# v with keys on partitions: block transposes on VectorE and moves between quadrants, in a two-layer encoder trunk

## The reference

```python
h = rms_norm(x, g); z = h @ w_in          # 1024 -> 3712
aq, ak, av, ag, bq, bk, bv, bg, ca, cb, cg = jnp.split(z, splits, axis=-1)
ya = neighbourhood_attention(aq, ak, av, rpb) * silu(ag)       # 4 heads, 8 x 16 window of an 8 x 64 grid
yb = dilated_attention(rotary(bq), rotary(bk), bv) * silu(bg)  # 6 heads, 3 dilated windows
yc = conformer_conv(ca, cb, ...) * silu(cg)                    # depthwise conv of 31 taps, 384 channels
x = x + concat([ya, yb, yc]) @ w_out
# an attention: p = softmax(q @ k.T * scale + bias); out = p @ v
```

## Time and profile before

| | us |
|---|---|
| median of 3 runs | 542.46 (540.92 to 544.98) |
| the profiled execution, its own time | 542.2 |
| its span, first to last instruction | 540.2 |
| busy: TensorE, VectorE, ScalarE, GpSimd | 528.5, 361.1, 287.3, 135.3 |
| granted clock of TensorE, mean | 0.999 of full speed |

### The profile page before, as it was taken

One profiled execution on the slowest core, in us unless ns is written; L12 is line 12 of the kernel. 1 busy time (PEld: TensorE's weight loads), 2 busy tenths in 40 slices (PEclk: granted clock), 3 DMA queues, 4 the chain that ended last, 5 costly groups with the idle time before them and its releaser, 6 DMA issues.

```text
span 540.2 us, 7426 instructions
## 1 busy us (share of the span) xinstructions
PE 528.5 (98%) x2684; PEld 416.0 (77%) x2684; DVE 361.1 (67%) x708; ACT 287.3 (53%) x546; POOL 135.3 (25%) x168
## 2 busy tenths in 40 slices
PE   7999999999999999999999999999999999999995
PEld 5788778687686888888888887877868778888884
DVE  5699798989773465521547959979999446554034
ACT  6433267667575566632533325856757566664223
POOL 0003232121132421333511223122111342223201
PEclk9999999999999999999999999999999999999999
DMA  8725687756474773799513369865595769689953
GB/s 263 280 75 133 147 188 181 165 128 152 103 163 110 161 184 69 177 246 306 142 36 99 102 133 225 204 136 131 141 175 122 178 130 207 126 163 235 227 88 157
DMA packets 47284, 86.26 MB, mean 160 GB/s; under 512 B 21264, under 2 KB 27280, under 8 KB 47248
## 3 DMA queue, kind: packets, MB, share of 16 engines
q0 software_dynamic: 17856, 61.09, 51.3%
q1 hardware_dynamic: 29392, 24.70, 15.5%
HBM read 78.43 MB, written 2.10 MB: 149 GB/s over the span
## 4 chain that ended last, share of the span: by engine, by line
PE 91%; DMA 4%; DVE 1%; ACT 1%; issue 1%; SPq 1%; POOL 1%; POOLq 0%; ACTq 0%
PE acc L484 21%; PE acc L486 20%; PE acc L485 20%; PE tp L590 5%; PE sc L576 5%; PE misc L618 4%; DMA w_hi<-w_in 2%; PE misc L624 1%; PE sc L528 1%; PE sc L484 1%; PE sc L486 1%; PE sc L485 1%; PE sc L529 1%; PE sc L530 1%; DMA sq<-sq 1%; PE misc L605 1%
## 5 line engine op out<-in xcount | busy, mean ns | idle before, releaser
L484 PE MATMUL acc<-act_hi,w_hi 128*128 128x512 f32 x496 | 202.5, 408 | 2.8 <-DVE act_lo L1221 2.6
L486 PE MATMUL acc<-act_lo,w_hi 128*128 128x512 f32 x496 | 194.2, 392 | 0.0
L485 PE MATMUL acc<-act_hi,w_lo 128*128 128x512 f32 x496 | 193.6, 390 | 0.0
L484 PEld LDWEIGHTS acc<-act_hi,w_hi 128*128 128x128 f32 x496 | 93.2, 188 | 28.4 <-issue 5.2
L486 PEld LDWEIGHTS acc<-act_lo,w_hi 128*128 128x128 f32 x496 | 93.1, 188 | 20.6
L485 PEld LDWEIGHTS acc<-act_hi,w_lo 128*128 128x128 f32 x496 | 93.4, 188 | 17.4 <-issue 0.5
L699 ACT ACTIVATE w_lo<-w_hi 128x1024 fp32r<-128x1024 f32 (+1 forms) x62 | 61.9, 998 | 48.0 <-DMA w_hi<-w_out 42.2
L762 ACT ACTIVATE prob<-prob,nmx 128x512 f32<-128x512 f32 (+1 forms) x80 | 50.6, 632 | 41.8 <-DVE nmx L1140 41.8
L787 ACT ACTIVATE pT<-tp 128x512 f32<-128x512 f32 (+1 forms) x80 | 40.6, 507 | 53.2 <-PE tp L590 52.8
L1120 DVE SCALAR_TENSOR_TENSOR y<-u,par,y 128x512 f32<-128x512 f32 x90 | 68.8, 764 | 0.0
L1120 DVE SCALAR_TENSOR_TENSOR acc<-u,par,acc 128x512 f32<-128x512 f32 x84 | 63.5, 756 | 0.0
(11 more groups left out here) (139 smaller groups left out, 717.8 us busy)
## 6 DMA issues: line engine op xcount, KB each, us to landing
w_hi<-w_in POOLq DMA_DIRECT2D x40, 512.0 KB, 4.1
w_lo<-w_in POOLq DMA_DIRECT2D x40, 512.0 KB, 5.7
pT<-w_in SPq DMA_DIRECT2D x17, 512.0 KB, 5.1
w_hi<-w_out POOLq DMA_DIRECT2D x16, 512.0 KB, 7.5
w_lo<-w_out POOLq DMA_DIRECT2D x16, 512.0 KB, 6.5
bias<-nabias SPq DMA_DIRECT2D x32, 128.0 KB, 3.2
sq<-sq SPq DMA_DIRECT2D x48, 64.0 KB, 2.8
x<-xT SPq DMA_DIRECT2D x8, 256.0 KB, 6.1
```

What stands on the lines that cost most here:

```text
L484: nc.tensor.matmul(to[:, :], w_hi[:, slot, k, :], a_hi[:, k, :], start=i == 0, stop=False)
L485: nc.tensor.matmul(to[:, :], w_lo[:, slot, k, :], a_hi[:, k, :], start=False, stop=False)
L486: last = nc.tensor.matmul(to[:, :], w_hi[:, slot, k, :], a_lo[:, k, :], start=False, stop=i == K - 1)
```

## The change

v is turned by VectorE and SyncE, in the way in which x was turned already. VectorE transposes `vT` in 32x32 blocks into `vB` (or into `zs`, for pair 1) right behind the emptying. SyncE then moves the 16 quadrants (i, j) to their places in `v`, one DMA each, in runs of 32 values (128 B), in the slots of `V_MOVES`. For a neighbourhood pair `v` holds 7 overlapping blocks of 128 keys, 64 apart, in place of 8 halves of windows. TensorE's rounds and ScalarE's copies go, and with them their uses of `misc`; `values` waits for the moves. The buffers `u` and `acc2` become one, `ub`, so that 4 tiles of x fit into it; x is turned in groups of 2, 4 and 2 tiles, and its moves make room for v's.

```diff
-        MISC_V = {0: [2], 1: [3], 2: [4], 3: [5, 6], 4: [10, 11]}
-        MISC_MEAN, MISC_LCOL, MISC_LBC = 7, 8, 9
-        MISC_L = 12
-        V_AT = {5: (0, 0), 13: (1, 0), 20: (2, 0), 22: (3, 0), 23: (3, 1), 32: (4, 0), 33: (4, 1)}
-        PAIRS_BEFORE = [0] * 3 + [1] + [2] * 4 + [3] * 4
-        USES_BEFORE = [3, 4, 8, 12, 12]
+        MISC_MEAN, MISC_LCOL, MISC_LBC = 2, 3, 4
+        MISC_L = 5
+        PAIRS_BEFORE = [0, 0, 2, 3, 3]
+        USES_BEFORE = [2, 2, 3, 5, 5]
...
-        X_BLOCKS = {16: range(0, 2), 26: range(2, 5), 36: range(5, KD)}
+        MOVED = 16 * len(QUADS)
+        V_MOVES = {3: (0, 0, 8), 5: (0, 8, 16)}
+        V_MOVES |= {11 + 4 * g + i: (1 + g, 4 * i, 4 * i + 4) for g in range(2) for i in range(4)}
+        V_MOVES |= {21 + 8 * g + i: (3 + g, 3 * i, min(3 * i + 3, 16)) for g in range(2) for i in range(6)}
+        X_TILES = [(0, 2), (2, 6), (6, KD)]
+        X_BLOCKS = {16: 0, 26: 1, 30: 2}
+        X_MOVES = {19: (0, 6), 20: (6, 12), 27: (12, 16)}
+        X_MOVES |= {35 + i: (16 + 4 * i, 20 + 4 * i) for i in range(5)}
+        X_AFTER = (36, 48)
...
+            def move_v(l, g, first, end):
+                if first == 0:
+                    sp.wait_ge(v_blocks, PAIRS * l + g + 1)
+                    if PAIRS * l + g >= 2:
+                        sp.wait_ge(pv_done, PAIRS * l + max(g - 1, 0))
                 for i, j in QUADS[first:end]:
+                    t = v_buf(g)[32 * i:32 * i + 32, :].rearrange("p (m z t) -> p m z t", z=4 if g < DPAIRS else 2, t=32)
+                    t = t[:, :, j, :] if g < DPAIRS else t[:, j // 2:j // 2 + NA_BLOCKS, j % 2, :]
+                    to = v[32 * j:32 * j + 32, g % 2, 0:QT if g < DPAIRS else NA_BLOCKS, 32 * i:32 * i + 32]
+                    sp.dma_start(to, t).then_inc(v_moved[g % 2], 16)
...
+                    if n in V_MOVES:
+                        move_v(l, *V_MOVES[n])
...
             def values(l, g):
 
                 pe.wait_ge(pt_ready, UNITS * l + UPP * (g + 1))
+                pe.wait_ge(v_moved[g % 2], MOVED * v_uses(l, g))
...
-                    if n in V_AT:
-                        turn_v(l, *V_AT[n])
...
-                    if n - 1 in V_AT:
-                        v_out(l, *V_AT[n - 1])
...
                     (scaled if kind == "bv" else scaled_by_column)(vT[:, :], c, 1.0).then_inc(acc_free, 1)
+                    dve.wait_ge(acc_free, emptied(l, c))
+
+                    before = {0: (l - 1, PAIRS - 1), 2: (l, 0), 3: (l, 2), 4: (l, 3)}.get(g)
+                    if before is not None and before[0] >= 0:
+                        dve.wait_ge(v_moved[before[1] % 2], MOVED * v_uses(*before))
+                    nc.vector.transpose(v_buf(g), vT[:, :]).then_inc(v_blocks, 1)
```

More of the change, by code:

```diff
@@ L84 @@
 NKEY = ROWS * NAW
+NA_STEP = P // 2
+NA_BLOCKS = (SEQ - P) // NA_STEP + 1
 NEG_TILE = 896
@@ L245, in build @@
         dve_own = sem("dve_own")
+        v_blocks = sem("v_blocks")
+        v_moved = [sem(f"v_moved{i}") for i in range(2)]
         x_blocks = sem("x_blocks")
@@ L360, in build, with v_buf, v_uses, na_block @@
         ROOTS = 2 * DEPTH
-        X_BLOCKS = {16: range(0, 2), 26: range(2, 5), 36: range(5, KD)}
         QUADS = [(i, j) for i in range(4) for j in range(4)]
-        X_MOVES = {n: (g, 2 * (n - first), 2 * (n - first) + 2) for g, first in enumerate((17, 27, 37))
-                   for n in range(first, min(first + 8, UNITS))}
-        N_MOVES = len(X_BLOCKS) * len(QUADS)
+        MOVED = 16 * len(QUADS)
[7 more added lines that the diff above has]
+        X_AFTER = (36, 48)
+        def v_buf(g):
+            return zs if g == 1 else vB[:, :]
+        def v_uses(l, g):
+            return (2 if g % 2 else 3) * l + g // 2 + 1
+        def na_block(b, half):
+            return ROWS * NA_LO[b] // NA_STEP + 2 * half
         def blocks(g):
-            return (u if g else cs)[:, :, :].rearrange("p j t -> p (j t)")
+            return ub[:, :] if g == 1 else cs[:, :, :].rearrange("p j t -> p (j t)")
         def row_x(a, half):
@@ L412, in swap, with move_x @@
                     sp.dma_start(zsw[32 * h:32 * h + 32, :], zs[o:o + 32, :]).then_inc(swap_in, 16)
[L414 to L418, removed]
-                for i, j in QUADS[first:end]:
+            def move_v(l, g, first, end):
[3 more added lines that the diff above has]
+                        sp.wait_ge(pv_done, PAIRS * l + max(g - 1, 0))
+                for i, j in QUADS[first:end]:
+                    t = v_buf(g)[32 * i:32 * i + 32, :].rearrange("p (m z t) -> p m z t", z=4 if g < DPAIRS else 2, t=32)
+                    t = t[:, :, j, :] if g < DPAIRS else t[:, j // 2:j // 2 + NA_BLOCKS, j % 2, :]
+                    to = v[32 * j:32 * j + 32, g % 2, 0:QT if g < DPAIRS else NA_BLOCKS, 32 * i:32 * i + 32]
+                    sp.dma_start(to, t).then_inc(v_moved[g % 2], 16)
+            def move_x(first, end):
+                for m in range(first, end):
+                    g, (i, j) = m // len(QUADS), QUADS[m % len(QUADS)]
+                    k0, k1 = X_TILES[g]
+                    if m % len(QUADS) == 0:
+                        sp.wait_ge(x_blocks, k1)
+                    to = x[:, k0:k1, :].rearrange("p k (a t) -> p (k a) t", t=P)
+                    t = blocks(g)[:, 0:(k1 - k0) * SEQ].rearrange("p (b t) -> p b t", t=P)
                     sp.dma_start(to[32 * j:32 * j + 32, :, 32 * i:32 * i + 32],
-                                 turned[32 * i:32 * i + 32, :, 32 * j:32 * j + 32]).then_inc(x_moved, 16)
+                                 t[32 * i:32 * i + 32, :, 32 * j:32 * j + 32]).then_inc(x_moved, 16)
             def load_bias(l, un):
@@ L624, in values @@
                                 last = nc.tensor.matmul(ob[HD * h:HD * (h + 1), b * P:(b + 1) * P],
-                                                        v[:, g % 2, 2 * b + half, HD * h:HD * (h + 1)],
+                                                        v[:, g % 2, na_block(b, half), HD * h:HD * (h + 1)],
                                                         pT[:, h, half, b * P:(b + 1) * P],
@@ L1098, in turn_blocks @@
                 elif g == 2:
-                    dve.wait_ge(x_moved, 16 * len(QUADS) * g)
-                for kk, k in enumerate(ks):
-                    nc.vector.transpose(blocks(g)[:, kk * SEQ:(kk + 1) * SEQ], x[:, k, :]).then_inc(x_blocks, 1)
+                    dve.wait_ge(x_moved, MOVED)
+                k0, k1 = X_TILES[g]
+                for k in range(k0, k1):
+                    nc.vector.transpose(blocks(g)[:, (k - k0) * SEQ:(k - k0 + 1) * SEQ], x[:, k, :]).then_inc(x_blocks, 1)
             def conv_taps(l, first, count):
```

26 lines of the change are left out of this document (11 added, 15 removed).

## The result

The changed kernel takes 548.68 us (median of 4 runs, 544.83 to 552.96), the kernel before beside it 541.69 (4 runs, 540.53 to 544.98): a ratio of 1.0123, 95% interval 1.0092 to 1.0154. It is slower by 7 us, where 3 us less were forecast, and outside the range. The profiled execution is the longest of the four, 552.96 us (span 550.9), so its losses are some 4 us larger than those of the median run; I use it for places and mechanisms and the medians for sizes.

A forecast was written before the change was run, and what follows sets the result against it. The prediction took TensorE, busy 528.5 of 540.2 us, as the bound. Its terms, -6.7 + 0.2 (layer 0) + 2.2 (layer 1) + 0.2 (values of pair 0) + 1.0 (tail) = -3.1 us, gave 539.1 us, range 535.4 to 544.5.

The forecast's parts named there:

- The failed step: SyncE's queue from slot 24 on: bias loads some 2 to 4 us later behind v's moves, costing TensorE nothing.
- The gross gain: TensorE: 14 rounds of four transposes removed, saving 6.7 us, 3.35 us a layer.
- Transposes: VectorE: ten added block transposes of 128x512, 0.7 us each, 3.5 us a layer, costing only where VectorE is already late.
- Turns 7 and 13 of layer 1: TensorE made late by the chain from the delayed swap of tile 11: a loss of 2.2 us.
- d: Delay of tile 11's swap behind v's first eight moves on SyncE: 1.2 us in layer 1, 1.0 in layer 0.
- Layer 0 at the same turns: The swap's delay mostly absorbed by 0.9 us of room and waits on VectorE: 0.2 us lost.
- DMA time: v's moves, 26,624 runs at 15.4 ns, use 26 us of each DMA engine, spread out and by itself hidden.
- Values of pair 0: TensorE's new wait for moved v before pair 0's value products: 0.2 us, up to 2.
- the tail: x's later moves fall where w_out is loaded, delaying weights for the row products: 1.0 us, bounds 0 and 3.5.
- (1): Rival: the swap's chain is not delayed and weights keep their time; 535.5 to 537.2 us, centre 536.3; chance 0.30.
- (2): Rival: short-run moves hold the swap's rows in the DMA queue; slower, 546.7 us with a delay of 5; chance 0.10.
- (3): Rival: the tail's weights chain is pushed by 3.5 us in place of 1.0; 541.6 us; chance 0.10.

The follow-up runs named there:

- e1: Changed kernel with the 32 loads of neighbourhood bias tables issued from ScalarE's queue in place of SyncE's: 539.09 us, ratio 0.9951 to the kernel before.
- e5: Changed kernel with only V_MOVES changed for pairs 3 and 4, so their moves go in other slots: 539.39 us, ratio 0.9958 to the kernel before.
- e11: Changed kernel without v's 160 moves, their waits and VectorE's 10 block transposes: 534.40 us, ratio 0.9865 to the kernel before.
- e10: Changed kernel without v's 160 moves and the waits on them, block transposes kept, v zeroed: 535.12 us, ratio 0.9889 to the kernel before.
- e9: Changed kernel with the edits of e1 and e5 together: 539.40 us, ratio 0.995 to the kernel before.
- e7: e2's two plain copies a pair, taken straight from vT without VectorE's ten block transposes: 539.68 us, ratio 0.997 to the kernel before.
- e3: Changed kernel with the same 160 transfers, each within its quadrant in 32 runs of 512 or up to 1024 B: 543.83 us, ratio 1.0032 to the kernel before.
- e2: Changed kernel with a pair's 16 moves replaced by two plain copies of rows: 539.12 us, ratio 0.9949 to the kernel before.
- e6: e1 with pair 0's 16 moves all in slot 5, behind tile 11's swap: 548.04 us, ratio 1.013 to the kernel before.
- e4: Changed kernel with pair 0's 16 moves all in slot 5, behind tile 11's swap: 550.81 to 559.18 us, ratio 1.0206 (first three runs) to the kernel before.
- e12: Kernel before with 160 moves of the same shapes added, between tiles nobody else uses: 556.82 us, ratio 1.0278 to the kernel before.

## Why the prediction was wrong

**The failed step.** It is the sentence "The bias loads stand behind v's moves on SyncE from slot 24 on, some 2 to 4 us later; TensorE meets the scores made of them a whole slot later, so nothing." Two things in it were wrong. The delay was 6 to 8 us where three moves, a wait for a transpose and three more moves stood ahead (6.3 and 8.2 us for units 32 and 33 above), and the cover was taken from the wrong row. What counts is the waiting instruction's queue: maxima with the reciprocal of the unit before behind them, thus ScalarE's norm, pT, and the next turn. The term is not 0 but +9.6 us, by after less e1, and e5 shows nearly the same (9.3) by order alone. Before's trace had it in view: VectorE waited there 5.7 us for these tables and ScalarE 10.6 for reciprocals, so the tables had no room. I had asked who stands behind a wait for the swap, and not for the tables.

**The gross gain.** Forecast 6.7, measured 7.15 (e11). Reading the distance of starts with and without a round was right; by tile starts the layers gain 3.3 and 4.0, where 3.35 each were forecast.

**Transposes.** 0.7 each forecast and 0.71 measured; of their time on VectorE only 0.7 us in all reached TensorE (e10 less e11).

**Turns 7 and 13 of layer 1.** d = 1.2 and a loss of 2.2 were forecast. Timeline after, against the earlier trace rows; before's times are to be taken 4.8 us later here, by which TensorE entered this layer late:

```profile
347.60 5.56 SPq L444 DMA_DIRECT2D v<-vB  x8
...
353.21 2.50 SPq L433 DMA_DIRECT2D sq<-sq  x4
...
361.78 1.29 POOL L963 TENSOR_TENSOR sq<-sq,cs 128x512 f32<-128x512 f32 x1 [6.40 <-DMA sq<-sq]
363.10 0.69 DVE L1101 TENSOR_TENSOR zc<-zc,sq 128x512 f32<-128x512 f32 x1 [3.98 <-POOL sq L963]
...
364.97 0.58 ACT L808 ACTIVATE pT<-tp 128x512 f32<-128x512 f32 x1
365.66 0.42 PEld L626 LDWEIGHTS tp<-ident,prob 128*128 128x128 f32 x4 [2.13 <-issue]
```

The eight moves end at 353.16 (0.7 us each) and the swap follows: 0.9 late; rotation, pT copy and turn are 1.2 late (361.78 against 355.74 + 4.8). VectorE's sum waits 3.98, not 2.55. It went step by step as written. Tile 17 stands 2.4 us later than tile 13, and in e11 0.4 earlier: a loss of 2.8 against 2.2. In the other executions with the same moves ahead of these turns it is 1.3 (e1), 2.3 (e9) and 2.8 (e5): the forecast lies among them. e10, with the transposes and no moves, loses 0.1 there, so d is the moves' alone and VectorE's 0.7 ahead of the swap hid itself.

**Layer 0 at the same turns.** 0.2 forecast; from e11's -0.8 to +0.9 it is 1.7. Against the earlier trace rows, timeline after, layer 0 and layer 1:

```profile
123.43 0.57 ACT L808 ACTIVATE pT<-tp 128x512 f32<-128x512 f32 x1
124.12 0.42 PEld L626 LDWEIGHTS tp<-ident,prob 128*128 128x128 f32 x4 [1.67 <-issue]
...
390.62 0.57 ACT L808 ACTIVATE pT<-tp 128x512 f32<-128x512 f32 x1
391.31 0.42 PEld L626 LDWEIGHTS tp<-ident,prob 128*128 128x128 f32 x4 [1.13 <-issue]
```

pT ends at 124.0, where it ended at 122.54: in this execution the delay came through and the 0.9 us of room were gone, +1.5 on the term. It isn't always so: against e11, e1 loses 0.2 here, as forecast, and e5 2.2. The term is mis-sized as a single number; it varies by 2 us from execution to execution.

**DMA time.** 26 us of each engine forecast from 15.4 ns a run; measured 108.5 less 83.7, 24.8. The price was right. "By itself that is hidden" was not: e7's table that landed in 9.9 us behind a bulk copy, and the 4.9 us between e3 and after, speak against it. How much the bytes alone cost is open, since e2's 3.6 us over e10 hold its late tables too; beside e10, e2's tiles lose some 1.3 us at the turns of layer 1 and 1.2 in its neighbourhood slots.

**Values of pair 0 and the tail.** 0.2 and 1.0 forecast. TensorE doesn't wait at the first in after, nor at the second (10.8 late before, 10.7 after). e6 shows how near the first is: eight moves later, 3.45 us.

**The rivals.** (1), the undelayed chain, is what e10 does, not after. (2) had the right queue and the wrong victim: the swap's rows don't wait long behind the moves (the rotation waited 6.40 for them, 5.98 before, and began 8.6 us after the swap's issue, 8.3 before); it is other loads that are issued late. What decided came ahead of the DMA engines, in SyncE's list; how packets are shared out, the rule of the Trainium skill ("DMA: Bandwidth & Descriptors") cited there, no run here shows. (3) didn't happen. That the forecast equals e1's time, 539.1, is in part luck: e1's gross gain was larger than forecast, it lost less at the turns and nothing in the tail, and still waited for tables.

## What to carry to other kernels

Before adding DMAs to an engine's queue, list every other load on that queue, and for each the instruction that waits for it and what stands behind that instruction on its engine; a load that the waits list already shows has no room. 0.6 us an issue is cheap for one DMA and dear for 160: if the queue can't be thinned, move the urgent loads to another one (e1) or place the moves where their source is ready, so that the queue stands less for them (e5). Mind the semaphore waits in the list as much as the issues: in e2, with 20 issues in place of 160, one such wait still made a table 4 us late. To price a change by parts, run the bare removal first (e11): it tells at once whether the gain or the cost was misjudged. And compare executions of the same code before reading a price of 1 or 2 us from two traces.

## What was not expected of the hardware

**TensorE's clock fell inside the work.** Before, the granted clock is 1.00 from 442 to 448 us. After, in windows of 3 us (busy us of PE, PEld, DVE, ACT, POOL, then PEclk, DMA share, GB/s):

```profile
443.00:446.00 3.00, 0.14 (x2) 0.17 (x2) 2.27 (x4) 1.56 (x4) 1.74 (x2) 1.00 0.13 22
446.00:449.00 3.00, 3.00 (x17) 2.41 (x17) 1.76 (x6) 2.16 (x8) 2.17 (x3) 0.54 0.29 25
449.00:452.00 3.00, 3.00 (x16) 2.41 (x15) 0.09 (x1) 1.26 (x3) 0.00 (x0) 0.89 0.98 220
```

TensorE had nothing to do for nearly 3 us (it waited 3.14 for pT), and the clock then was at half, 1.2 GHz, until about 449.6; products start 0.43 us apart there and 0.23 elsewhere. It happened before at 211 us (0.50 over 3 us, after a wait of 2.28), and in e6 after its wait of 3.45 us (0.58 from 105 to 108). In the profiled executions of e4, e7 and e12 it fell too: in e7 to 0.56 from 458 to 461, after a wait of 3.34. Half speed from about 446.2 to 449.6 costs up to 1.7 us on top of the wait itself. The traces of before, e1, e2, e3, e9, e10 and e11 have no such stretch inside the work.

The mean granted clock of a whole run was 0.990 to 0.995 in after's four runs and 0.996 to 0.998 in e1's six; an estimate from these means is that some 2 us of the 9.6 between the two are the clock's. It does not explain the wide spread of after's runs: 552.96, 546.95, 550.42 and 544.83 us had 0.992, 0.990, 0.995 and 0.994.

**Landing times vary widely.** The answer on line 461, the bias tables, all of one size, after:

```profile
DMA to landing us min/median/max: 2.1/3.4/7.2
```

and on line 427 before:

```profile
DMA to landing us min/median/max: 2.0/3.2/7.1
```

The spread is no work of the change: before, the table issued at 439.2 took 7.1 us and VectorE waited 2.5 for it, though it had been issued as soon as its buffer was free. What the change adds is late issue on top. No run here separates what makes a landing long.
